# Which expert slots VectorE adds into the residual: every third instead of every fifth in the first three prompt tiles of a hybrid decoder step

## What is computed

```python
e = i1[ci // 16] * NK + i2[ci % 16]            # 8 heads x 16 experts for each token
gate = softmax(sc)
h = einsum('td,thkd->thk', xb, u[e])
w = gate * gelu(h)
y = einsum('thk,thkd->td', w, v[e])            # and then: hp = hp + y
```

## Time and profile before

| | us |
|---|---|
| median of the runs | 2407.39 |
| lowest and highest of 3 | 2406.6, 2416.46 |
| the profiled execution | 2401.09 |
| its span, first to last instruction | 2399.3 |
| slots of tile 0, from about | 545 |
| slots of tile 1, from about | 943 |
| slots of tile 2, from about | 1350 |
| slots of tile 3, from about | 1760 |
| slots of tile 4, from about | 2230 |

### The profile page before, as it was taken

How to read it: one execution, slowest core, us unless ns; L and a number is a source line. 1 busy time by engine, 2 the same in 40 slices (tenths; PEclk the granted TensorE clock), 3 DMA queues, 4 the chain that set the end, 5 groups by cost and what they waited for, 6 DMA issues and landing times.

```text
span 2399.3 us, 20324 instructions
## 1 busy us (share of the span) xinstructions
PE 1851.8 (77%) x6178; PEld 913.0 (38%) x6178; DVE 1386.0 (58%) x2954; ACT 772.6 (32%) x2325; POOL 747.0 (31%) x641
## 2 busy tenths in 40 slices
PE   3987889686776888776788777678868788776777
PEld 3443435463333354342345443334522222353211
DVE  1124453338755568875656886565766543568744
ACT  2122222213325335333423433343333322233333
POOL 2001001113333434333343433344422222444432
PEclk9998899788999899898899998899988898899999
DMA  6346651258899999889799997989999999999998
GB/s 187 112 151 236 223 185 40 105 194 313 322 372 356 408 421 419 319 327 393 303 417 421 390 333 294 374 339 422 421 413 332 361 400 368 398 421 419 405 420 347
DMA packets 149127, 784.44 MB, mean 327 GB/s; under 512 B 15969, under 2 KB 24689, under 8 KB 71306
## 3 DMA queue, kind: packets, MB, share of 16 engines
q0 software_dynamic: 83680, 605.56, 63.7%
q1 hardware_dynamic: 62578, 172.70, 19.4%
q10 hardware_dynamic: 2760, 4.88, 0.6%
HBM read 767.11 MB, written 16.26 MB: 326 GB/s over the span
## 4 chain that ended last, share of the span: by engine, by line
PE 38%; DMA 26%; DVE 20%; ACT 9%; issue 3%; SPq 2%; POOL 1%; ACTq 0%; DVEq 0%; POOLq 0%
DMA sb_uv<-in_peer_uv,sb_eidx 21%; PE bank L1920 16%; PE bank L1580 7%; DVE sb_uv L1540 7%; DMA sb_xin<-pre_conv 3%; PE bank L1834 2%; PE bank L1813 2%; PE bank L1868 2%; DVE sb_hres L1516 2%; ACT sb_diag L1164 2%; PE bank L1892 1%; ACT sb_ew L1157 1%; DMA sb_zone<-in_cache_kT 1%; DVE sb_xin L1229 1%; ACT sb_gel L1153 1%
## 5 line engine op out<-in xcount | busy, mean ns | idle before, releaser
L1920 PE MATMUL bank<-sb_uv,sb_diag 128*128 128x512 f32 (+1 forms) x1800 | 979.1, 678 | 424.3 <-ACT sb_diag L1164 404.1
L837 POOL DMA_INDIRECT sb_uv<-in_peer_uv,sb_eidx x576 | 688.5, 1195 | 1178.1 <-PE bank L1920 892.6
L1540 DVE CUSTOM_DVE_ANT_0 sb_uv<-sb_uv,sb_xn 128x1024 f32<-128x1024 f32 x576 | 697.3, 1220 | 295.2 <-DMA sb_uv<-in_peer_uv,sb_eidx 293.5
L1920 PEld LDWEIGHTS bank<-sb_uv,sb_diag 128*128 128x128 f32 (+1 forms) x1800 | 330.2, 201 | 942.0 <-ACT sb_diag L1164 603.2
L1153 ACT ACTIVATE sb_gel<-sb_h 128x1 f32<-128x1 f32 x576 | 116.1, 202 | 938.3 <-DVE sb_h L1540 931.2
L1580 PE MATMUL bank<-sb_w,sb_xnT 128*128 128x512 f32 (+1 forms) x560 | 265.1, 623 | 13.7 <-DMA sb_w<-in_w_in 8.5
L1516 DVE SCALAR_TENSOR_TENSOR sb_hres<-sb_uv,sb_ew,sb_hres 128x1024 f32<-128x1024 f32 x126 | 161.4, 1281 | 60.8 <-ACT sb_ew L1157 60.7
L1164 ACT ACTIVATE sb_diag<-sb_stay,sb_ew 128x128 f32<-128x128 f32 (+1 forms) x450 | 177.2, 394 | 42.8 <-ACT sb_ew L1157 1.9
L1157 ACT ACTIVATE sb_ew<-sb_gel,sb_gate 128x1 f32<-128x1 f32 x576 | 169.7, 295 | 19.8
L1892 PEld LDWEIGHTS bank<-sb_rT,sb_zone 128*128 128x128 f32 x1280 | 156.5, 196 | 28.6 <-issue 28.6
L1892 PE MATMUL bank<-sb_rT,sb_zone 128*128 128x128 f32 x1280 | 158.2, 279 | 2.3 <-issue 2.3
(11 more groups left out here) (302 smaller groups left out, 1566.6 us busy)
## 6 DMA issues: line engine op xcount, KB each, us to landing
sb_zone<-in_w_route SPq DMA_DIRECT2D x20, 2304.0 KB, 12.3
sb_zone<-in_w_mixer SPq DMA_DIRECT2D x10, 2048.0 KB, 16.6
sb_zone<-in_cache_kT SPq DMA_DIRECT2D x64, 256.0 KB
sb_zone<-in_cache_v SPq DMA_DIRECT2D x64, 256.0 KB
sb_xn<-in_conv_w SPq DMA_DIRECT2D x15, 1024.0 KB
sb_w<-in_w_in SPq DMA_DIRECT2D x14, 1024.0 KB, 8.4
sb_xin<-pre_conv SPq DMA_DIRECT2D x48, 256.0 KB
sb_uv<-in_peer_uv,sb_eidx POOLq DMA_INDIRECT x576
```

Source lines behind the costliest of these rows:

```text
L837: nc.gpsimd.indirect_dma_start(uv[:, m % RING, :], None, i["peer_uv"], bass.IndirectOffsetOnAxis(ap=eidx[:, t % 2, n:n + 1], axis=0)).then ...
L1540: nc.vector.tensor_tensor_reduce(out=uv[:, m % RING, 0:D], in0=uv[:, m % RING, 0:D], in1=xn2[:, t % 2, :], scale=1.0, scalar=0.0, op0=ALU. ...
L1920: ins = nc.tensor.matmul(bank[half][0:rows, :], lhsT=G["diag"][:, d % DIAGS, 0:rows], rhs=uv[:, m % RING, D + 512 * half:D + 512 * half + ...
```

## The change

`added_here` decides slot by slot. In tiles 0 to 2 the slots with n % 3 == 2 (2, 5, 8, ... 125: 42 per tile) are added, where it was n % 5 == 4 (4, 9, ... 124: 25 per tile). Slots 14, 29, 44, 59, 74, 89, 104 and 119 are in both sets. In tile 3 (n % 5 in 1 and 4) and tile 4 (none) nothing changes. Nothing else is edited, but all that asks `added_here` follows: the waits for the ring on GpSimd, the order key there, the diagonals and their numbering on ScalarE and TensorE, and the adds on VectorE.

```diff
         def added_here(m):
             t, n = ALL[m]
-            return t < PT and (n % 5 == 4 or t + 1 == PT and n % 5 == 1)
+            return t < PT and (n % 3 == 2 if t + 1 < PT else n % 5 in (1, 4))
```

## The result

The changed kernel takes 2433.05 us (median, 2428.58 to 2436.85) beside 2408.41 us for the kernel before: a ratio of 1.0091, 95% interval 1.0074 to 1.0107. It is slower by 25 us where 2388 was forecast. Its profiled execution took 2434.7 us with a span of 2432.6. The profiled execution of the kernel before, 2401.09 us, is 7 us under its median, so stretches summed against it can come out a little too long.

What follows compares the result with a forecast made beforehand. The bound was taken to change by stretch: gathers at 420 GB/s, elsewhere chains between engines. Attention -22.5, state update -2.4, tail +4.5 and gathers +1.5 gave about -19 us: 2388 from a median of 2407.4, range 2366 to 2413.

Steps and rivals of the forecast that it cites:

- state-update term: Slots 1 to 46: 1.2 us per tile lost to adds, 2 us gained by moved slots, -2.4 us over three tiles.
- add count: First half of the state update: five new adds exposed where four were, +1.2 us per tile.
- Slots 38 and 39 swap: State update, second half: frees a ring place earlier, ahead of attention; part of 2 us gained per tile.
- Rival 3: TensorE's clock falls in attention, four more folds per tile at half clock cost 22 us: no change, 2410; chance 0.11.
- Attention: Slots 50 to 73: VectorE's waits for scores and rsqrt shrink, fewer folds stand ahead of the mixer; -22.5 us.
- Tail: Slots 110 to 127, VectorE picking the next tile's experts: six adds where there were four, 1.5 us per tile, +4.5.
- Gathers' issue: GpSimd issues gathers more slowly beside VectorE's adds, touching perhaps 17 more issues: +1.5 us in all.
- rival 1: VectorE becomes the bound in slots 4 to 27 and 110 to 127: 18 us of adds, attention gain lost, 2425; slower, 0.14.
- Rival 2: Transfers hide the attention gain, as mixer and router weights join the same queue: no change, 2402 to 2410; chance 0.15.
- rival 4: State-update stretch shortens too, by removed folds in its chain, another 3 x 5 us: 2373; chance 0.12.

Runs made afterwards that it cites:

- e13: Kernel before with one added slot in each of tiles 0 to 2 moved by one, 35 for 34: 2421.83 us, ratio 1.0047.
- e7: Kernel before plus six zero-valued VectorE adds in each of tiles 0 to 2, no fold taken away: 2411.79 us, ratio 1.0015.
- e8: Kernel before with the folds of six slots in each of tiles 0 to 2 cut to 8 columns of each half: 2422.85 us, ratio 1.0056.
- e3: New pattern only in slots 75 to 127 of tiles 0 to 2, old one elsewhere: 2413.16 us, ratio 1.0007 to the kernel before.
- e2: New pattern only in slots 46 to 74 of tiles 0 to 2, old one elsewhere: 2396.37 us, ratio 0.9941 to the kernel before.
- e1: New pattern only in slots 0 to 45 of tiles 0 to 2, old one elsewhere: 2437.74 us, ratio 1.0107 to the kernel before.
- e9: Changed kernel with two added slots in each of tiles 0 to 2 put back, 34 for 35 and 39 for 38: 2410.10 us, 0.9983 of before.
- e5: Kernel before with its nine added slots among 0 to 45 of tiles 0 to 2 moved to places of the new pattern: 2436.09 us, ratio 1.0119.
- e15: Changed kernel with two zero-weight matmuls of 512 columns at slot 44 in each of tiles 0 to 2: 2431.28 us, 1.0092 of before.
- e10: Changed kernel with two zero-weight matmuls of 512 columns in place of slot 35's fold in tiles 0 to 2: 2414.71 us, 1.0007 of before.

## Why the prediction was wrong, point by point

**What failed: the state-update term, -2.4 us, bounds 15 lost to 18 gained over three tiles.** Measured alone it is +26 us. The method was to ask which slot stands just *ahead* of a step, and its answers held in the main: slot 32 added ahead of the state product gives 2.3 us (2.2 forecast), slot 34 as a fold ahead of the read-out takes 0.6 of them in the changed kernel (1.7 where slot 32 is not added, e13). What was never asked is what stands *behind* a step whose answer TensorE then waits for. The fold of 35 was the only work TensorE had while VectorE, and then ScalarE, went from the read-out to the next diagonal. "Slots 38 and 39 swap, which frees a ring place earlier" counted the ring and left out GpSimd's rsqrt between two gathers, though the same step was priced rightly in attention; it cost 1.5 us by slot 40 and nothing in the end. In the first half, the add count (+1.2 us per tile) was too small as well: slots 0 to 32 of tile 0 are 7.6 us longer, about half of it with the adds alone (e7, 3.7) and half with the cut folds alone (e8, 3.8). The bounds excluded the result because both ends were made of adds; no end had a link at half clock in it.

**Rival 3 had the cause and the wrong place.** It took the 3.78 us record of the earlier trace rows, four more such folds per tile, 22 us, and set them in the attention stretch, where they would only cancel a gain. There the clock went from 0.89 to 0.86. In the state update it went from 0.91 to 0.82, and attention's gain stayed. Its count was off as well: one fold, one state product and eight groups of output products per tile at half clock are 4.8 us, and the ring that runs dry behind them makes it more. The Trainium skill ("TensorE: Matmul & The Clock Gate", "HAM oscillation — how this bites in real kernels") describes the clock falling in waits between short bursts of matmuls, there waits for DMA. The traces agree in kind, with a wait for a diagonal of ScalarE: 3.17 us idle, then 3.78 us for what takes 1.98.

**Attention, -22.5: right in kind, too large.** Alone it gives 14 us (10 to 18). The waits at L1380 and for the rsqrt went as forecast; VectorE's waits after, window 700:800:

```profile
DVE sb_rz L1388 <- ACT sb_S L1039: 10.7, 4, 3.1
DVE sb_ams L1399 <- ACT sb_xn L1058: 5.3, 1, 5.3
DVE sb_hres L1405 <- POOL sb_ars L815: 0.9, 1, 0.9
DVE sb_S L1380 <- PE bank L1782: 0.2, 1, 0.2
```

Before, the same four were 8.4, 3.0, 3.9 and 8.4 us. The first two had no place in the sum: 2.3 us each came back as waits for ScalarE. The rsqrt stands ahead of gather 75, as forecast (GpSimd's timeline after):

```profile
785.59 1.27 POOL L815 TENSOR_TENSOR sb_ars<-sb_ams,sb_minus_half 128x4 f32<-128x4 f32 x1
787.04 1.00 POOL L837 DMA_INDIRECT sb_uv<-in_peer_uv,sb_eidx  x1 [0.19 <-issue]
```

**Tail, +4.5: in kind.** VectorE is busy 43.23 of 44 us there, 98% where 95% was foretold, and slots 75 to 127 are 0.4, 2.5 and 2.7 us longer. Measured alone (e3) the kernel is 2 us slower, inside an interval of 5 us each way.

**Gathers' issue, +1.5, and rival 1.** Single issues reach 3.01 us in the changed kernel's state update, but six extra adds of the same form per tile (e7) cost 0.15%, with 1 inside the interval. VectorE did not become the bound of the state update: it is busy 110.72 us of 545:690 where it was 110.24. The mark given for rival 1, state-update stretches over 4 us longer, came true for another reason; the clock, read in the same window, would have told the two apart. Rival 2 needs attention's gain to vanish, which e2 excludes; rival 4 is excluded by e1.

## What to carry to other kernels

When work is taken off TensorE in an in-order schedule, lay the removed pieces over its timeline and ask of each what TensorE would do in its place: if the answer is "wait", add the next links of the chain at the slow clock's durations, which the trace usually shows somewhere. A pattern such as every third is never only a count: here two slots out of 42 made the difference between 0.9% slower and no slower than before (e9). And a cheap test of a suspected clock loss is filler work that depends on nothing, at the gap, with the same filler at another place beside it.

## What the runs showed of the hardware

- Taking matmul columns away, and nothing else, made the kernel slower: e8, 1.0056 with 18 folds cut short to 8 columns of each half.
- An idle stretch of 3.17 or 3.18 us on TensorE behind the last read-out was followed by half clock every time: in after, e1, e5, e13 and e15, three tiles each, the fold behind it took 3.40 to 3.78 us. With 1.02 to 1.26 us of it left, in the other 13 kernels, the same fold took 1.98 or 1.99. How long the spell lasted differed (state product 2.07 or 1.16 us), and why is open. The length of the gap is not all that counts: fold 56 of the kernel before took 3.78 us behind 1.41 us of idle time, and in e8 a fold did so with none right in front of it.
- Three pairs of matmuls by a zero weight, 12 records of 0.5 us in a kernel of 2.4 ms, were worth 18 to 20 us against the changed kernel (e10), and nothing nine slots later (e15).
- An issue of a gather on GpSimd took 0.95 us alone and up to 3.01 beside VectorE's row operations; the six added instructions per tile of e7 cost nothing that can be told.
